# Rows for the residual gates: ten pairs of DMAs through DRAM instead of products with the unit matrix

## The reference

```python
mx = jnp.split((silu(c) @ w_mod[l] + b_mod[l])[:, None, :], 9, axis=-1)    # nine vectors of 1024
mz = jnp.split(silu(c_ctx) @ w_mod[l] + b_mod[l], 9, axis=-1)
x = x + 0.5 * mx[2] * swiglu(modulate(rms_norm(x), mx[0], mx[1]), ffn1_w1[l], ffn1_w3[l], ffn1_w2[l])
z = z + 0.5 * mz[2] * swiglu(...)
...
x = x + mx[5] * (mix_x @ w_out[l])
x = x + 0.5 * mx[8] * swiglu(...)
if not last: z = z + mz[5] * (mix_z @ w_out[l]); z = z + 0.5 * mz[8] * swiglu(...)
```

## Time and profile before

| | |
|---|---|
| median of three runs | 3114.86 us (3114.34 to 3119.23) |
| the profiled execution: span from the first to the last instruction | 3110.6 us; the profile gives no other time of it |
| TensorE busy with matmuls | 3000.5 us, 96% |
| VectorE, ScalarE busy | 1788.4 us, 1470.9 us |
| mean granted TensorE clock | 0.992 |
| DMA | 556.64 MB, mean 179 GB/s |
| the first block's part of the span | to about 2000 us |

### The profile page before, as it was taken

The page is one execution under the profiler, slowest core; times in us unless marked ns, Lnnn a source line. Parts: engine busy times, 40 slices in busy tenths (PEclk is TensorE's granted clock), DMA queues, the critical chain, the costliest instruction groups (busy, mean ns, idle before and its releaser), DMA issues.

```text
span 3110.6 us, 53816 instructions
## 1 busy us (share of the span) xinstructions
PE 3000.5 (96%) x23104; PEld 2751.1 (88%) x23104; DVE 1788.4 (57%) x2773; ACT 1470.9 (47%) x2182; POOL 153.9 (5%) x147
## 2 busy tenths in 40 slices
PE   7999999999999999999999989999999999999998
PEld 6899788898889998899898789999899999989997
DVE  5445555655556545455655555464756656585665
ACT  4344444453555443344454444455654445565443
POOL 0000000001000000000200000001110101110000
PEclk9999999999999999999999999999999999999999
DMA  7765445654555555765365445554355655435563
GB/s 286 281 230 168 153 160 198 211 188 135 168 190 172 185 184 204 262 220 175 110 183 164 151 162 190 188 166 136 119 166 187 201 189 160 128 119 168 171 199 132
DMA packets 409689, 556.64 MB, mean 179 GB/s; under 512 B 25276, under 2 KB 357996, under 8 KB 409068
## 3 DMA queue, kind: packets, MB, share of 16 engines
q1 hardware_dynamic: 409452, 553.20, 53.2%
HBM read 552.12 MB, written 1.05 MB: 178 GB/s over the span
## 4 chain that ended last, share of the span: by engine, by line
PE 82%; DVE 9%; ACT 3%; issue 3%; DMA 2%; SPq 0%; POOL 0%; DVEq 0%; ACTq 0%
PE psum L119 24%; PE psum L121 23%; PE psum L120 23%; PE psum L711 1%; DVE wl L2180 1%; DVE wl L277 1%; PE psum L1920 1%; DMA wr<-in_ffn_w_dram 1%; PE psum L2345 1%; PE psum L1542 1%; PE psum L1194 1%; PE psum L2429 1%; PE psum L127 1%; PE psum L1529 1%; ACT probs L2470 1%
## 5 line engine op out<-in xcount | busy, mean ns | idle before, releaser
L277 DVE TENSOR_TENSOR wl<-wr,wh 128x1024 fp32r<-128x1024 f32 (+1 forms) x558 | 658.0, 1215 | 226.0 <-ACT wh L266 224.9
L266 ACT ACTIVATE wh<-wr 128x1024 fp32r<-128x1024 f32 (+1 forms) x558 | 554.7, 1039 | 229.3 <-DMA wr<-in_ffn_w_dram 207.6
L119 PE MATMUL psum<-xt_hi,wh 128*128 128x256 f32 (+1 forms) x2000 | 564.6, 282 | 4.3 <-DVE wl L277 3.0
L121 PE MATMUL psum<-xt_hi,wl 128*128 128x256 f32 (+1 forms) x2000 | 557.2, 279 | 0.0
L120 PE MATMUL psum<-xt_lo,wh 128*128 128x256 f32 (+1 forms) x2000 | 557.1, 279 | 0.0
L2180 DVE TENSOR_TENSOR wl<-wr,wh 128x1024 fp32r<-128x1024 f32 (+3 forms) x336 | 390.3, 1197 | 119.0 <-ACT wh L2172 118.1
L119 PEld LDWEIGHTS psum<-xt_hi,wh 128*128 128x128 f32 (+1 forms) x2000 | 376.4, 188 | 16.0 <-issue 8.1
L120 PEld LDWEIGHTS psum<-xt_lo,wh 128*128 128x128 f32 (+1 forms) x2000 | 376.0, 188 | 2.3
L121 PEld LDWEIGHTS psum<-xt_hi,wl 128*128 128x128 f32 (+1 forms) x2000 | 376.9, 188 | 0.1
L2172 ACT ACTIVATE wh<-wr 128x1024 fp32r<-128x1024 f32 (+3 forms) x336 | 323.2, 999 | 99.9 <-DMA wr<-in_mlp_w_dram 73.0
L119 PE MATMUL psum<-wh,xt_hi 128*128 128x256 f32 (+1 forms) x1280 | 364.8, 285 | 2.4 <-ACT vv L3336 1.9
(11 more groups left out here) (465 smaller groups left out, 5343.1 us busy)
## 6 DMA issues: line engine op xcount, KB each, us to landing
wr<-in_ffn_w_dram SPq DMA_DIRECT2D x231, 1024.0 KB, 5.2
wr<-in_w_in_dram SPq DMA_DIRECT2D x88, 1024.0 KB, 5.1
wr<-in_w_mod_dram SPq DMA_DIRECT2D x72, 1024.0 KB, 4.9
wr<-in_mlp_w_dram SPq DMA_DIRECT2D x64, 1024.0 KB, 5.1
wr<-in_w_out_dram SPq DMA_DIRECT2D x20, 1024.0 KB, 4.9
wr<-in_mem_w_kv_dram SPq DMA_DIRECT2D x8, 1024.0 KB, 4.8
wr<-in_w_branch_dram SPq DMA_DIRECT2D x16, 512.0 KB, 3.4
wr<-in_w_branch_dram SPq DMA_DIRECT2D x8, 1024.0 KB, 4.8
```

What stands on the lines that cost most here:

```text
L119: pe.matmul(out, a[0], b[0], start=first, stop=False)
L121: return pe.matmul(out, a[1], b[0], start=False, stop=last)
L266: act.activation(self.high[s][:, r], self.raw[s][:, r], ACT.Copy).then_inc(self.highs.sem, 1)
L277: dve.tensor_tensor(self.low[s][:, r], self.raw[s][:, r], self.high[s][:, r].bitcast(F32), ALU.subtract).then_inc(self.lows.sem, 1)
```

## The change

The eight products and the two copies go from all ten down pieces, and with them the two units that each claimed. A new class `GateRows` issues two DMAs from SyncE per gate: `write` puts the [128, 8] columns into one row of a new DRAM tensor (1,024 single numbers of 4 bytes: in SBUF every second one, for the streams lie side by side; in DRAM 512 bytes apart for one partition), and `read` brings the row of 4 KB onto all 128 partitions. `write` is in the `fetch` of the same down piece, `read` in that of the second piece after it. The consumers wait for the landing of the read.

```diff
@@ class DownPiece
-    def spread(self, mod, part, v, rows, room=None):
-        self.rows, self.n_units = (mod, part, v, rows, room), 2
...
     def pe(self, pe, step):
...
         wv = w.split(pe, self.m)
         beat = Beat(step, 8, self.steps)
-        if self.rows:
-            mod, part, v = self.rows[:3]
-            mod.wait_part(pe, part)
-            for j in range(2):
-                bank = w.claim(pe, self.u0 + j)
-                w.touch()
-                for k in range(4):
-                    col = mod.columns(part, 4 * j + k, v).to_broadcast([P, P])
-                    last = pe.matmul(bank[:, k * P:(k + 1) * P], col, w.eye, start=True, stop=True)
-                last.then_inc(self.spread_ready.sem, 1)
         pe.wait_ge(f_.g_lo.sem, f_.g_lo.at(i + 1))
...
-    def late(self, name, eng):
-        f_, w = self.ffn, self.w
-        if self.rows and name == "act":
-            rows, room = self.rows[3:]
-            if room:
-                room(eng)
-            for j in range(2):
-                u = self.u0 + j
-                eng.wait_ge(self.spread_ready.sem, self.spread_ready.at(j + 1))
-                eng.activation(rows[:, j * 512:(j + 1) * 512], w.ps[:, 6 + u % 2, :], ACT.Copy).then_inc(w.bank_free[u % 2].sem, 1)
+class GateRows:
+    def __init__(self, w, mod, part, v, row, rows, room=None):
+        self.w, self.mod, self.part, self.v, self.row, self.rows, self.room = w, mod, part, v, row, rows, room
+        self.written, self.landed = w.share("gate_row_written", 1, 16), w.share("gate_row_landed", 1, 16)
+    def write(self, sp):
+        self.mod.wait_part(sp, self.part)
+        col = self.mod.b["mod"][self.mod.l][:, self.part * KT:(self.part + 1) * KT, self.v]
+        with self.w.nc.allow_non_contiguous_dma(reason="a column of every partition"):
+            sp.dma_start(self.row.rearrange("o (k p) -> p (o k)", p=P), col).then_inc(self.written.sem, 16)
+    def read(self, sp):
+        if self.room:
+            self.room(sp)
+        sp.wait_ge(self.written.sem, self.written.at(1))
+        sp.dma_start(self.rows[:, :], self.row.to_broadcast([P, D])).then_inc(self.landed.sem, 16)
+    def rows_in(self, eng):
+        eng.wait_ge(self.landed.sem, self.landed.at(1))
...
+    gate_dram = nc.dram_tensor("gate_rows_dram", (10, D), F32, kind="Internal").ap()
...
-    zf1.down[8].spread(mods[0], 2, Z.v, rows1)
+    g_zf1_8 = spread(zf1.down[8], mods[0], 2, Z.v, rows1)
...
     w.queue(order)
+    for piece, g in spreads:
+        piece.fetch.append(g.write)
+        w.pieces[piece.m + 2].fetch.append(g.read)
```

More of the change, by code:

```diff
@@ L839, in __init__ @@
         super().__init__(ffn.w, src)
-        self.ffn, self.i, self.rows = ffn, i, None
-    def spread(self, mod, part, v, rows, room=None):
-        self.rows, self.n_units = (mod, part, v, rows, room), 2
-        self.spread_ready = self.w.share("gate_spread", 2)
-        return self
-    def rows_in(self, eng):
-        for j in range(2):
-            self.w.emptied(eng, self.u0 + j)
+        self.ffn, self.i = ffn, i
     def pe(self, pe, step):
@@ L3728, in first_block, with spread @@
     zeroed = w.share("gate_w_zero", 1)
+    gate_dram = nc.dram_tensor("gate_rows_dram", (10, D), F32, kind="Internal").ap()
+    spreads = []
+    def spread(piece, mod, part, v, rows, room=None):
+        n = len(spreads)
+        g = GateRows(w, mod, part, v, gate_dram[n:n + 1, :], rows, room)
+        spreads.append((piece, g))
+        return g
     def gate_loads(l, room):
@@ L3923, in first_block @@
     zf1.down[0].after(x_t0)
-    zf1.down[8].spread(mods[0], 2, Z.v, rows1)
+    g_zf1_8 = spread(zf1.down[8], mods[0], 2, Z.v, rows1)
     order += weave(zf1.pieces, M0[8:20], 1, 2)
-    z_r1 = Residual(w, zf1, rows1, zf1.down[8].rows_in, Z.x, Z.ss, rtmp)
+    z_r1 = Residual(w, zf1, rows1, g_zf1_8.rows_in, Z.x, Z.ss, rtmp)
     z_t3 = turn(Z, 0, 3, z_r1.wait_squares, 6)
@@ L3933, in first_block @@
     xf1.down[0].after(z_t3)
-    xf1.down[6].spread(mods[0], 2, X.v, rows1, z_r1.wait_added)
-    xf1.down[8].spread(mods[0], 5, Z.v, rows2)
+    g_xf1_6 = spread(xf1.down[6], mods[0], 2, X.v, rows1, z_r1.wait_added)
+    g_xf1_8 = spread(xf1.down[8], mods[0], 5, Z.v, rows2)
     tail = weave(xf1.pieces[3:], M0[20:36], 0, 2)
@@ L3949, in first_block @@
     background += [zm.st] + zm.head_turns() + zm.attention()
-    x_r1 = Residual(w, xf1, rows1, xf1.down[6].rows_in, X.x, X.ss, rtmp)
+    x_r1 = Residual(w, xf1, rows1, g_xf1_6.rows_in, X.x, X.ss, rtmp)
     x_t3 = turn(X, 0, 3, x_r1.wait_squares, 6)
@@ L3959, in out_projection @@
         return p_
-    z_out = out_projection(0, Z, zm, xf1.down[8].rows_in)
+    z_out = out_projection(0, Z, zm, g_xf1_8.rows_in)
     order += z_out.pieces
@@ L3971, in first_block @@
     zf2.pieces[0].after(z_t6)
-    zf2.down[1].spread(mods[0], 5, X.v, rows2, z_out.wait_added)
-    zf2.down[4].spread(mods[0], 8, Z.v, rows1, x_r1.wait_added)
+    g_zf2_1 = spread(zf2.down[1], mods[0], 5, X.v, rows2, z_out.wait_added)
+    g_zf2_4 = spread(zf2.down[4], mods[0], 8, Z.v, rows1, x_r1.wait_added)
     xm = Mixers(X, 0, x_in)
@@ L3982, in first_block @@
     background += xm.attention(xm.beside.wait_done)
-    x_out = out_projection(0, X, xm, zf2.down[1].rows_in)
+    x_out = out_projection(0, X, xm, g_zf2_1.rows_in)
     cut = body.index(zf2.down[8])
@@ L3988, in first_block @@
     background += [After(w, x_out.last), sq_x2, x_t6]
-    z_r2 = Residual(w, zf2, rows1, zf2.down[4].rows_in, Z.x, Z.ss, rtmp)
+    z_r2 = Residual(w, zf2, rows1, g_zf2_4.rows_in, Z.x, Z.ss, rtmp)
     z_t7 = turn(Z, 1, 0, z_r2.wait_squares, 6)
@@ L3995, in first_block @@
     xf2.down[0].after(z_t7)
-    xf2.down[4].spread(mods[0], 8, X.v, rows1, z_r2.wait_added)
+    g_xf2_4 = spread(xf2.down[4], mods[0], 8, X.v, rows1, z_r2.wait_added)
     order += xf2.pieces
@@ L3999, in first_block @@
     xf2.pieces[6].fetch.append(layer_in[1].fetch)
-    x_r2 = Residual(w, xf2, rows1, xf2.down[4].rows_in, X.x, X.ss, rtmp)
+    x_r2 = Residual(w, xf2, rows1, g_xf2_4.rows_in, X.x, X.ss, rtmp)
     x_t7 = turn(X, 1, 0, x_r2.wait_squares, 3)
@@ L4008, in first_block @@
     xf3.pieces[0].after(x_t7)
-    xf3.down[6].spread(mods[1], 2, X.v, rows1, x_r2.wait_added)
+    g_xf3_6 = spread(xf3.down[6], mods[1], 2, X.v, rows1, x_r2.wait_added)
     order += weave(xf3.pieces, M1[16:24], 3, 3)
-    x_r3 = Residual(w, xf3, rows1, xf3.down[6].rows_in, X.x, X.ss, rtmp)
+    x_r3 = Residual(w, xf3, rows1, g_xf3_6.rows_in, X.x, X.ss, rtmp)
     x_t8 = turn(X, 1, 3, x_r3.wait_squares, 6)
@@ L4015, in first_block @@
     zf3.down[0].after(x_t8)
-    zf3.down[4].spread(mods[1], 2, Z.v, rows1, x_r3.wait_added)
-    zf3.down[7].spread(mods[1], 5, X.v, rows2, x_out.wait_added)
+    g_zf3_4 = spread(zf3.down[4], mods[1], 2, Z.v, rows1, x_r3.wait_added)
+    g_zf3_7 = spread(zf3.down[7], mods[1], 5, X.v, rows2, x_out.wait_added)
     x_in1 = InProjection(w, A["w_in"][1], X.pair, X.h, gate_t(X, 1), x_t8.wait_done)
@@ L4027, in first_block @@
         zf3.pieces[asked + i].fetch.append(lambda sp, i=i: xm1.bias_in.fetch(sp, i, 9))
-    z_r3 = Residual(w, zf3, rows1, zf3.down[4].rows_in, Z.x, Z.ss, rtmp)
+    z_r3 = Residual(w, zf3, rows1, g_zf3_4.rows_in, Z.x, Z.ss, rtmp)
     z_t9 = turn(Z, 1, 3, z_r3.wait_squares, 3)
@@ L4086, in first_block @@
     order += M1[26:34]
-    x_out1 = out_projection(1, X, xm1, zf3.down[7].rows_in)
+    x_out1 = out_projection(1, X, xm1, g_zf3_7.rows_in)
     order += x_out1.pieces
@@ L4095, in first_block @@
     xf4.pieces[0].after(x_t9)
-    xf4.down[6].spread(mods[1], 8, X.v, rows1, z_r3.wait_added)
+    g_xf4_6 = spread(xf4.down[6], mods[1], 8, X.v, rows1, z_r3.wait_added)
     order += xf4.pieces
-    x_r4 = Residual(w, xf4, rows1, xf4.down[6].rows_in, X.x, None, rtmp)
+    x_r4 = Residual(w, xf4, rows1, g_xf4_6.rows_in, X.x, None, rtmp)
     urgent += [After(w, xf4.pieces[-1]), x_r4]
```

## The result

The changed kernel takes 3126.74 us (median of 13 runs, 3117.48 to 3129.75) against 3115.03 us for the kernel before (13 runs, 3112.46 to 3123.73, beside it on the same chips): a ratio of 1.0025, with a 95% interval of 1.0017 to 1.0032. It is slower, by 8 us by the ratio and by 12 us by the medians, where 19 us less had been forecast, and it lies outside the range. The third rival, 3123 us, is nearest to what happened.

The account below looks back on a forecast made before the run. TensorE was taken to bound the kernel (busy 96% of the span, 82% of the last chain). Terms 18.5 + 0.4 + 1.1 - 0.5 - 0.5 = 19.0 us; 3114.9 - 19.0 = 3096 us, range 3091 to 3110.

Parts of the forecast that it names:

- The third rival: On SyncE's queue: write slow as the gain reads (11.4 us), costing 27 us against 19; 3123 us, chance 0.10.
- The step that failed: On SyncE's queue: each write was nearest to quick 128-byte load pieces and would take 1 to 3 us.
- the upper bound from the gain reads: On SyncE's queue: at the gain reads' pace of 11 ns a piece, the write's 1,024 pieces take 11.4 us.
- The removal: On TensorE and ScalarE: dropping products and copies gains 18.5 us, plus waits of 0.4 and 1.1 us.
- The 1.85 us per gate: On TensorE at ten down pieces: removing the products saves 1.85 us each, 18.5 us in all.
- the 1.5 us of waits in my sum: Bank waits gone: 0.4 us at zf2.down[1], 1.1 us at a modulation piece at 848.78 us.
- The copies and L711: On ScalarE: 20 copies cost at 0, except a 1.15 us bank wait near 848 us that goes, worth 1.1 us.
- The read: On SyncE's queue: 512 KB onto all partitions adds about 2 us, in a hole; its consumer comes over 15 us later.
- The tight places: At xf1.down[8] and zf1.down[8], crowded DMA or a gain read ahead: 0.5 us given back at each.
- what a late load costs: At the gain reads: 8.8 us late cost TensorE 1.22 us; a load 2 us late costs nothing there.
- The signs: Of being wrong: loads at 12 us and more, DMA share under 0.2, new `wl` waits, SyncE waiting, a residual waiting.
- two readings: For the write: strided rule read as the slow pace (third rival), or a 10.5 ns packet floor giving 0.67 us.

Follow-up runs that it names:

- no_rows: The changed kernel with neither products nor writes nor reads, except the first read into each of two buffers, from input c; 3101.97 us, ratio 0.9953.
- turned: The changed kernel with one product per gate turning all eight columns, one ScalarE copy, a write of eight 512-byte pieces, later reads; 3101.66 us, ratio 0.9943.
- no_write: The changed kernel without its ten writes; the reads stay but take a row of input c, true gates left out; 3103.8 us, ratio 0.9958.
- far_write: As no_write, but with writes of the same 1,024 single numbers, each 128 bytes from the next in DRAM; 3104.25 us, ratio 0.9963.
- near_write: As no_write, but with writes of 1,024 single numbers into the same 4 KB, each partition's eight side by side; 3134.34 us, ratio 1.0051.

## Why the prediction was wrong

**The step that failed** is the size of one term: "The write's pieces all have sources of their own, so it is nearest to the 128 byte pieces: I take 1 to 3 us in the queue." In the queue, from its first packet to its landing, the write took 8.2 us (12.1 us from its issue, for a load of 1 MB is ahead of it); the upper bound from the gain reads was 11.4 us. The first load behind a write landed after 11.9 us (median of ten) instead of 5.2 us. I took the difference between the quick and the slow small transfers to be how many different places they read from. The runs show that for writes it is how many pieces share a short stretch of DRAM. That fact stood in the text, as one clause for the third rival, and it got 0.10.

**The trace had no row that bore on it**, since the kernel before stores nothing in small pieces. The only slow row of small pieces had 23 GB/s, at a DMA share of 0.09. The loads behind the write ran at the same 23 GB/s, at a share of 0.22. It deserved more than a tenth when the alternative was a row of a read with pieces 32 times as long. Whether the gain reads are slow by the same mechanism, many pieces on one 256 byte run, no run here tells.

**The removal: 14.6 us, not 20.0.** The 1.85 us per gate is right as a local figure. In the profiles the clock took part of it back. The span of no_rows is 13.3 us shorter than before's; its idle time is 0.6 us less, and it loses 6.4 us more to the clock: 18.5 + 0.6 - 6.4 = 12.7 us, nearly all of the 13.3. But only 1.6 of the 6.4 us lie where the gates are; 1.5 us fall in the first 60 us and 3.3 us behind 2000 us, and turned, which has the products away too, loses only 2.4 us more than before. Matmul for matmul, L865 left out, no_rows is 2.4 us behind the kernel before at 58 us and 14.3 us ahead at 2008 us, so it gains 16.7 us over the stretch with the gates. The idle time there is 0.6 us longer, not shorter, so the 1.5 us of waits in my sum (0.4 and 1.1) were not gained in all. That the lower clock comes from TensorE's running ahead, with its waits at other places, is not shown; two profiles can differ by such a sum. I had priced waits by their length alone. In no_write, 2.9 us more of wait at the softmax of 789 us comes on top (3.23 us against 0.36).

**The copies and L711.** Right: in the source view of L711 after, the wait for L896 is gone. **The read.** Right: nothing measurable. **The tight places.** I had put 0.5 us each; with a write that takes 12 us, xf1.down[8] cost a wait of 6.32 us and zf1.down[8] one of 3.33 us. The third rival had 6.6 us for each.

**The third rival's own sum** was 27 us for the writes and 19 us for the gain, slower by 8. Measured are 22.5 us (spans of after and no_write) and 14.6 us less what reads cost, slower by 8 (ratio) to 12 (medians). Its net was right by luck, with both parts some 4 us too high, and its write of 11.4 us was longer than the 8.2 us that the write took. Its warning that SyncE would stand at the read's wait came true in the trace, with 29.3 us, and cost nothing. By its threshold, "a write of some 11 us", 8.2 us should have cost less than the products. So what a late load costs was too low as well: I had taken 1.22 us for a load 8.8 us late, from one place of the trace, and nothing for the half-clock stretch behind a wait. The loads also stay late after the landing: the last write landed at 1990.3 us, and the full rate came at 1993 us.

**The signs** that I had named as wrong, all but one, were there: loads at 12 us and more behind most writes with the DMA share at 0.22 (I had said under 0.2), `wl` waits behind a gate, SyncE at the write's landing. Of the two readings of the Trainium skill's "DMA: Bandwidth & Descriptors" that I had weighed, the rule of its section "Rules for kernel authors" against a strided last dimension pointed the right way, and the floor per packet of its section "Measured" did not lead to the cost: the packets take 9 ns each, in agreement with about 10.5 ns, but the time goes behind them. Neither says what decides: far_write breaks the same rule, with as many single numbers, and costs nothing.

**Open.** The late load at 777 us; why the writes cost 12.8 us beside the products and 20.9 us without them (by the ratios); and what in the chip holds the engines. The runs show the condition and the size, not the place.

## What to carry to other kernels

Before a DMA scatters single numbers, ask where they land: numbers written side by side as separate pieces held the DMA engines for some 6 to 8 us a time here, 256 of them as long as 1,024, and the same numbers 16 bytes or more apart, or gathered first by one product into pieces of 512 bytes, cost nothing that could be told. If no row of the trace has the operation at all, let the bound that comes from the nearest slow row have a chance to match, for a stall of the DMA engines is paid by every load behind it. Read a landing time with what was queued ahead: 3.9 of the 12.1 us here had passed before the write's first packet, behind a load. And price a new wait of TensorE with the half-clock stretch that may come with it, not by its length alone.

## What the runs showed of the hardware beyond expectation

- Separate 4-byte pieces next to each other in DRAM: landing 12.1 us, some 3.9 us of it before the first packet, behind the load ahead; 8 bytes apart 8.4, 16 apart 6.8, 32 apart 6.7, 128 apart 6.1; 128 pieces of 32 bytes 5.1 us. Whether one partition's numbers are neighbours or 32 partitions' made no difference (12.9 us), nor did the queue (12.5 us), nor a quarter of the count (12.5 us).
- Meanwhile the engines moved 20 to 23 GB/s with loads of 1 MB queued, and near_write's reads, of a row of `c`, landed late as well (13.9 us against 7.4 us in no_write). The packets of the write themselves are recorded as short (9 ns), and the stall is seen only behind them. From 1985.0 to 1986.5 us the 16 engines together started one packet, with a load in the queue; the 113 packets of that load in 1984 to 1989 us took 158 ns each on average and up to 1.46 us, where packets of the same 1,024 bytes take 46 ns at full rate. The busy share alone (0.22) hides this; rate and landing times show it.
- Waits of TensorE of 3.33 and 6.32 us each came with 6.7 us at half the clock, which cost 2.9 and 1.6 us on top of the waits. A wait of 3.50 us at 37.19 us, in the kernel before, came with no such stretch. Over the run the added idle time of 16.9 us came with 11.9 us more lost to the clock, 3.1 us of it unrelated to the change.
